# Decoder trunk on one core: the MoE blocks' gather and combine take fp32 operands whole, in place of two float32r pieces, and the table of extra passes is written early from ACT's queue

## What is computed

```python
scores = jax.nn.sigmoid((x @ router_w).astype(jnp.float32))
...
_, idx = lax.top_k(masked, TOP_K)
gate = jnp.take_along_axis(scores, idx, -1)
gate = gate / jnp.sum(gate, -1, keepdims=True) * ROUTED_SCALE
```

## Time and profile before

| | |
|---|---|
| median of 3 runs | 1443.56 us (1441.83 to 1446.32) |
| profiled execution, its own time | 1440.45 us |
| span of its trace | 1438.7 us |
| mean granted TensorE clock | 0.968 |
| PE busy | 1345.1 us, 93% of the span |
| DVE, ACT busy | 424.6 us, 317.4 us |
| DMA over the span | 310 GB/s, 446 MB |

### The profile page before, as it was taken

How to read it: one execution, slowest core, us unless ns; L and a number is a source line. 1 busy time by engine, 2 the same in 40 slices (tenths; PEclk the granted TensorE clock), 3 DMA queues, 4 the chain that set the end, 5 groups by cost and what they waited for, 6 DMA issues and landing times. The chain is left out here.

```text
span 1438.7 us, 16559 instructions
## 1 busy us (share of the span) xinstructions
PE 1345.1 (93%) x6265; PEld 672.7 (47%) x6265; DVE 424.6 (30%) x897; ACT 317.4 (22%) x670; POOL 18.2 (1%) x92
## 2 busy tenths in 40 slices
PE   7897889999999999999959879999999999999985
PEld 5665855343444434444325545544344343443432
DVE  2465527222221222212134234712212122121213
ACT  2354223111111111111112231311112111121111
POOL 1001000000000000000000000000000000000000
PEclk9998999999999999999989999999999999999997
DMA  9215025799999999999944522488999999999990
GB/s 348 91 36 206 1 77 215 283 376 397 418 417 417 419 416 419 417 418 418 415 169 154 191 109 97 195 337 364 408 417 418 418 417 419 418 417 419 416 383 32
DMA packets 93651, 446.24 MB, mean 310 GB/s; under 512 B 9972, under 2 KB 12455, under 8 KB 60327
## 3 DMA queue, kind: packets, MB, share of 16 engines
q1 hardware_dynamic: 93606, 445.64, 76.9%
HBM read 444.57 MB, written 1.05 MB: 310 GB/s over the span
## 5 line engine op out<-in xcount | busy, mean ns | idle before, releaser
L363 PE MATMUL psum<-w_up_ring,moe_x_selected 128*64 128x512 f32 x2048 | 455.0, 597 | 16.4 <-issue 16.4
L363 PEld LDWEIGHTS psum<-w_up_ring,moe_x_selected 128*64 128x64 f32 x2048 | 148.5, 138 | 311.0 <-issue 311.0
L426 PE MATMUL psum<-w_down_ring,moe_hT 128*64 128x512 f32 x1024 | 233.9, 598 | 0.9 <-ACT moe_hT L705 0.9
L887 DVE SCALAR_TENSOR_TENSOR moe_h<-moe_silu,moe_slot_gate,psum 128x256 f32<-128x256 f32 x64 | 30.7, 480 | 398.6 <-ACT moe_silu L698 398.6
L426 PEld LDWEIGHTS psum<-w_down_ring,moe_hT 128*64 128x64 f32 x1024 | 67.9, 136 | 134.4 <-issue 133.0
L698 ACT ACTIVATE moe_silu<-psum 128x256 f32<-128x256 f32 x64 | 24.6, 384 | 426.4 <-PE psum L363 426.4
L418 PE MATMUL psum<-moe_out_high,moe_matchT 128*128 128x512 f32 x256 | 113.9, 445 | 0.0
L905 DVE TENSOR_TENSOR moe_out_low<-psum,moe_out_high 128x512 fp32r<-128x512 f32 x64 | 44.3, 692 | 232.7 <-ACT moe_out_high L710 232.7
L376 PE MATMUL psum<-moe_match,moe_x_high 128*128 128x512 f32 x256 | 108.6, 424 | 0.0
L418 PE MATMUL psum<-moe_out_low,moe_matchT 128*128 128x512 f32 x256 | 101.3, 396 | 0.0
L376 PE MATMUL psum<-moe_match,moe_x_low 128*128 128x512 f32 x256 | 101.0, 395 | 0.0
(11 more groups left out here) (490 smaller groups left out, 1115.7 us busy)
## 6 DMA issues: line engine op xcount, KB each, us to landing
w_up_ring<-in_moe_w_gate SPq DMA_DIRECT2D x128, 1024.0 KB, 11.2
w_up_ring<-in_moe_w_up SPq DMA_DIRECT2D x128, 1024.0 KB, 13.3
w_down_ring<-in_moe_w_down SPq DMA_DIRECT2D x128, 1024.0 KB, 12.6
w_up_ring<-in_ev_w_in SPq DMA_DIRECT2D x4, 2048.0 KB, 12.2
w_up_ring<-in_od_w_in SPq DMA_DIRECT2D x4, 2048.0 KB, 10.4
w_up_ring<-in_ev_w_out SPq DMA_DIRECT2D x2, 2048.0 KB, 9.6
w_up_ring<-in_od_w_out SPq DMA_DIRECT2D x2, 2048.0 KB, 7.6
ln_gain_bias<-in_ln_g SPq DMA_DIRECT2D x4, 512.0 KB, 9.0
```

What stands on the lines that cost most here:

```text
L363: last = nc.tensor.matmul(k.psum[e * SLOTS:(e + 1) * SLOTS, 6, :], xsel[:, kk, own:own + SLOTS], up_view(slots[e], kk), start=kk == 0, sto ...
L426: last = nc.tensor.matmul(k.psum[e * SLOTS:(e + 1) * SLOTS, bank, :], hT[:, j * P + e * SLOTS:j * P + (e + 1) * SLOTS], k.w_down[slots[e]] ...
```

## The change

The pieces go. Gather reads `k.x` itself, every eighth column of a row of 1024 as the operand of 128 columns, and `match` becomes fp32. Combine reads one fp32 tile `y`, whose first half ACT copies out of bank 4 and whose second half DVE copies out of bank 7, each as soon as its own half of `pe_down` is done. `matchT` becomes fp32. `high_part` and `low_part` are dropped. The table is written to DRAM from ACT's DMA queue after the first pair, and read back from the same queue after the second; SP only waits for it where it did before. The loops for extra passes change in the same way and are left out here.

```diff
@@ pe_gather
-                for part in (x_high, x_low):
-                    last = nc.tensor.matmul(k.psum[:, 4 + kk % 2, :], part[:, t, kk, :],
-                                            match[:, t, :, :].rearrange("p e s -> p (e s)"),
-                                            start=t == 0 and part is x_high, stop=t == NT - 1 and part is x_low)
+                last = nc.tensor.matmul(k.psum[:, 4 + kk % 2, :], k.x[:, t, kk:D:KD],
+                                        match[:, t, :, :].rearrange("p e s -> p (e s)"), start=t == 0, stop=t == NT - 1)
@@ pe_combine
-            for o in (high, low):
-                last = nc.tensor.matmul(k.psum[:, 2 * t + half, :], matchT[:, i, t * P:(t + 1) * P],
-                                        o[:, half * BANK:(half + 1) * BANK], start=begin and o is high, stop=True,
-                                        skip_group_check=True)
+            last = nc.tensor.matmul(k.psum[:, 2 * t + half, :], matchT[:, i, t * P:(t + 1) * P],
+                                    y[:, half * BANK:(half + 1) * BANK], start=begin, stop=True, skip_group_check=True)
@@ sync
-            sp.wait_ge(s.table_sb, 1)
-            sp.dma_start(k.over_dram, table_i[:]).then_inc(s.table_dram, 16)
-            sp.wait_ge(s.table_dram, 16)
-            sp.dma_start(back_i[:].rearrange("p b c -> p (b c)"),
-                         k.over_dram.rearrange("b c -> (b c)").unsqueeze(0).to_broadcast([P, MAX_OVER * 4])
-                         ).then_inc(s.table_back, 16)
             sp.wait_ge(s.table_back, 16)
@@ tensor
-            pe.wait_ge(s.parts, NT)
             pe.wait_ge(s.match, 1)
             pe_gather(0, NT)
@@ tensor, pair
-                    pe.wait_ge(s.low_a, p)
-                    pe.wait_ge(s.low_b, p)
+                    pe.wait_ge(s.out_a, p)
+                    pe.wait_ge(s.out_b, p)
@@ scalar
-            high_part(0)
             take_xT(1)
             scores(0)
-            high_part(1)
             scores(1)
@@ scalar, pair
-                nc.scalar.copy(high[:, 0:BANK], k.psum[:, 4, :]).then_inc(s.high_a, 1)
-                act.wait_ge(s.down_b, p + 1)
-                nc.scalar.copy(high[:, BANK:], turn_ps).then_inc(s.high_b, 1)
+                nc.scalar.copy(y[:, 0:BANK], k.psum[:, 4, :]).then_inc(s.out_a, 1)
 
-            for i in range(4):
+            pair(0, 0, first=True)
+            act.wait_ge(s.table_sb, 1)
+            act.dma_start(k.over_dram, table_i[:]).then_inc(s.table_dram, 16)
+            pair(0, 1, first=True)
+            act.wait_ge(s.table_dram, 16)
+            act.dma_start(back_i[:].rearrange("p b c -> p (b c)"),
+                          k.over_dram.rearrange("b c -> (b c)").unsqueeze(0).to_broadcast([P, MAX_OVER * 4])
+                          ).then_inc(s.table_back, 16)
+            for i in (2, 3):
                 pair(0, i, first=True)
@@ vector
-            low_part(0)
             group_heads(0)
-            low_part(1)
             group_heads(1)
@@ vector, pair
-                dve.wait_ge(s.high_a, p + 1)
-                nc.vector.tensor_tensor(low[:, 0:BANK], k.psum[:, 4, :], high[:, 0:BANK], ALU.subtract).then_inc(s.low_a, 1)
-                dve.wait_ge(s.high_b, p + 1)
-                nc.vector.tensor_tensor(low[:, BANK:], turn_ps, high[:, BANK:], ALU.subtract).then_inc(s.low_b, 1)
+                dve.wait_ge(s.down_b, p + 1)
+                nc.vector.tensor_copy(y[:, BANK:], turn_ps).then_inc(s.out_b, 1)
```

More of the change, by code:

```diff
@@ L309, in output_and_experts @@
     shared_w = at("shared_weights", [P, 2, KD, FE], F32, SHARED_OFFSET)
[L310 to L313, removed]
+    y = at("out", [P, D], F32, SHARED_OFFSET)
+    matchT = at("matchT", [P, 4, S], F32, SHARED_OFFSET + 4 * D)
+    hT = at("hT", [P, KF * P], F32, SHARED_OFFSET + 8 * D)
     shared_wd = k.mixT[:].rearrange("p (j c) t -> p j (c t)", j=KF)
@@ L344, in output_and_experts @@
     back_i = sb("back_i", [P, MAX_OVER, 4], I32)
-    back = at("back", [P, MAX_OVER, 4], F32, SHARED_OFFSET + 13 * D)
-    shifted = at("shifted", [P, NT, 2], F32, SHARED_OFFSET + 14 * D)
+    back = at("back", [P, MAX_OVER, 4], F32, SHARED_OFFSET + 9 * D)
+    shifted = at("shifted", [P, NT, 2], F32, SHARED_OFFSET + 10 * D)
     up_ps, turn_ps = k.psum[:, 6, :], k.psum[:, 7, :]
@@ L384, in pe_gather_two @@
             for t in range(NT):
[L385 to L388, removed]
+                last = nc.tensor.matmul(k.psum[:, bank, c * P:(c + 1) * P], k.x[:, t, 4 * (bank - 4) + c:D:KD],
+                                        match[:, t, 0:2, :].rearrange("p e s -> p (e s)"), start=t == 0, stop=t == NT - 1)
         return last
@@ L614, in _ @@
             shared_down(1, 0)
-            pe.wait_ge(s.low_a, PAIRS)
-            pe.wait_ge(s.low_b, PAIRS)
+            pe.wait_ge(s.out_a, PAIRS)
+            pe.wait_ge(s.out_b, PAIRS)
             with pe.If(n_over < 1):
@@ L643, in _ @@
                     pe_down((2, 3), 1, 7).then_inc(s.v_down, 1)
-                    pe.wait_ge(s.v_low, 2 * i + 2)
+                    pe.wait_ge(s.v_out_a, i + 1)
+                    pe.wait_ge(s.v_out_b, i + 1)
                     pe_combine(0, 0)
@@ L663, in take_xT @@
                                    k.psum[:, 4 + b, :].rearrange("p (c n) -> p c n", c=4)).then_inc(s.xT, 1)
-            def high_part(t):
-                act.wait_ge(s.normed1, t + 1)
-                nc.scalar.copy(x_high[:, t], k.x[:, t, :].rearrange("p (c k) -> p k c", k=KD)).then_inc(s.x_high, 1)
             def scores(t):
@@ L733, in _ @@
                     act.wait_ge(s.v_down, i + 1)
-                    nc.scalar.copy(high[:, 0:BANK], k.psum[:, 4, :]).then_inc(s.v_high, 1)
-                    nc.scalar.copy(high[:, BANK:], turn_ps).then_inc(s.v_high, 1)
+                    nc.scalar.copy(y[:, 0:BANK], k.psum[:, 4, :]).then_inc(s.v_out_a, 1)
             nc.scalar.activation(w.early[:], w.ln_eps[:], ACT.Sqrt)
@@ L778, in _ @@
                 scale_shifted(nc, k, w1, t).then_inc(s.normed1, 1)
-            def low_part(t):
-                dve.wait_ge(s.x_high, t + 1)
-                dve.wait_ge(s.normed1, t + 1)
-                nc.vector.tensor_tensor(x_low[:, t], k.x[:, t, :].rearrange("p (c k) -> p k c", k=KD), x_high[:, t],
-                                        ALU.subtract).then_inc(s.parts, 1)
             def group_heads(t):
@@ L946, in _ @@
                                                    ALU.mult).then_inc(s.v_h, 1)
-                    dve.wait_ge(s.v_high, 2 * i + 2)
-                    nc.vector.tensor_tensor(low[:, 0:BANK], k.psum[:, 4, :], high[:, 0:BANK], ALU.subtract).then_inc(s.v_low, 1)
-                    nc.vector.tensor_tensor(low[:, BANK:], turn_ps, high[:, BANK:], ALU.subtract).then_inc(s.v_low, 1)
+                    dve.wait_ge(s.v_down, i + 1)
+                    nc.vector.tensor_copy(y[:, BANK:], turn_ps).then_inc(s.v_out_b, 1)
             dve.wait_ge(s.tables, 32)
```

10 lines of the change are left out of this document (4 added, 6 removed).

## The result

The changed kernel takes **1612.09 us**, the median of 4 runs (1611.05 to 1613.57). The kernel before took 1442.69 beside it (4 runs, 1440.41 to 1446.32). The ratio is **1.1172**, 95% interval 1.1146 to 1.1198: slower by 11.7%. The forecast of 1606 was 6 us low, and the range of 1592 to 1630 holds the time.

What follows compares the result with a forecast made beforehand. PE was taken to bound the kernel, with the DMA only just following. Gather +93.3, combine +92.8, router -0.4 and block ends -16.4 and -4.6 sum to +164.7 on a 1438.7 us span; forecast 1606 us, range 1592 to 1630.

Steps and rivals of the forecast that it cites:

- PE sets the pace: Steady MoE loop: PE, full through a 59.87 us cycle, is the bound; the DMA at 420 GB/s only just follows.
- Rival 4: MoE loop: the DMA sets the pace, so added PE work partly vanishes in hidden waits; 1590 us with a tenth gone; chance 0.05.
- Gather, +93.3: Gather: 16 fp32 matmuls of 0.859 us plus 0.1 fill, 13.84 against 8.01 us; 16 gathers add 93.3 us.
- Combine, +92.8: Combine: two fp32 halves take 3.60 us a pair against 2.15; over 64 pairs this adds 92.8 us.
- The router's choice, -0.4: Ahead of the router's choice: dropping high_part and low_part saves 0.2 us a layer, 0.4 in all.
- The ends of the blocks, -16.4 and -4.6: Last pair's pe_up in each block: the early table removes 16.4 us of idle time and 4.6 us of slow clock.
- The doubt that the last weights would be late: Block ends: weights still coming until about 1400 might be late next; the whole gain was taken, other bound 12 us.
- rival 3: Block ends: the gain stays out because PE waits for last weights or ACT's queue; about 1626 us; chance 0.06.
- ACT, 0: ACT's queue in the first quad: the table's write lands before the silu of pair 2, so the move costs 0.
- Rival 1: Gather and combine: fp32 records run at the pieces' pace, 0.25 us, giving about 1419 us; chance 0.02.
- Rival 2: Gather: strided weight loads of 32-byte step take up to 748 ns, adding 163 us, about 1769 us; chance 0.04.
- The sum: Whole kernel: 93.3 + 92.8 - 0.4 - 16.4 - 4.6 = +164.7 us of span.

Runs made afterwards that it cites:

- whole_packed: Changed kernel, but gather reads x from a packed fp32 copy made on ACT, so weight loads are contiguous: 1612.38 us.
- pieces_early_table: Kernel before with only the table moved, written and read back early on ACT's queue; gather and combine keep float32r pieces: 1419.50 us, ratio 0.9831.
- pieces_strided: Kernel before with x's two float32r pieces in x's own order, so gather loads every eighth column: 1450.83 us, ratio 1.0057.

## Why the prediction was right, step by step

**PE sets the pace.** Right. After the change PE is busy for all 72.08 us of a cycle and the DMA at 0.87. Rival 4 fell: no part of the added work went into hidden waits, since the halves' 6.04 and 6.16 add up to the cycle's 12.21.

**Gather, +93.3.** The mechanism was right, two records of 0.43 us for each fp32 product; the size was slightly off. A gather takes 14.06 us and not 13.84, so 14 of them cost 6.05 more each. The first of each block costs 5.39 more (242.41 to 250.84 before, 242.44 to 256.26 now). Together 95.5, and the kernel with gather's edit alone has 95.4. The 0.22 that was missed lies at a gather's start. The first gather of a block, whose first load begins 0.43 us ahead of its first record (242.01 and 242.44), takes 13.82 us, 0.08 over 32 records. The others start behind `pe_up` with load and record together and take 0.24 more, or 0.11 more where the loads are packed (whole_packed, 13.93). So the strided load accounts for 0.13 of it; the forecast's 0.1 for filling the array stood for all the rest, which is 0.19.

**Combine, +92.8.** This was the term that missed most. The halves came as forecast (1.82 and 1.81, so 3.63 against a forecast 3.60), but the price of a pair was worked out from 2.15, the halves alone. From the start of combine to `pe_down` a pair took 1068.50 - 1065.98 = 2.52 and takes 1184.19 - 1180.11 = 4.08: +1.56, of which 1.48 in the halves and 0.08 in the transposes between them, which now take 0.45 instead of 0.37. Over a quad the mean is 6.16 / 4 = 1.54, and 64 pairs make 98.6, where the experiment has 99.2. I had let the work between the halves out of the sum because its instructions didn't change; its length did.

**The router's choice, -0.4.** The gain came, though the first gather starts at 242.44 us and started at 242.41 before. PE's timeline before, in the first block:

```profile
239.78 0.23 PE L528 MATMUL psum<-moe_sel_bf,before_bf 128*128 128x64 bf16 x2 [0.23 <-DVE moe_sel_bf L816]
...
242.41 0.80 PE L376 MATMUL psum<-moe_match,moe_x_high 128*128 128x512 f32 x1
243.05 0.40 PE L376 MATMUL psum<-moe_match,moe_x_low 128*128 128x512 f32 x1
```

and in the changed kernel:

```profile
239.41 0.22 PE L513 MATMUL psum<-moe_sel_bf,before_bf 128*128 128x64 bf16 x2
```

From the start of the shared expert's ten records to the choice PE took 5.96 us and takes 5.61; in the second block 5.73 and 5.57. Together that is 0.5 for the forecast 0.4. The cover was not whole: in the first block PE idled 0.23 us for DVE, which is gone. The first record of the old gather stands 0.64 us ahead of the second, where records come every 0.23, so its recorded start is some 0.4 early. That is why the gain doesn't show there, and why the first gathers seem to cost 5.39 and not 5.8: the gain is inside the 95.5.

**The ends of the blocks, -16.4 and -4.6.** Right: 21.0 forecast, and pieces_early_table has 21.5 by the span (23 to 26 by the medians, since the profiled execution of the kernel before is one of its fastest). Both `pe_up` are back at 7.04 us. The doubt that the last weights would be late was unfounded, even at the DMA's full pace. That the gain stays out (rival 3) fell. But the gain belongs to the kernel before: with combine whole, a late table costs 4 to 5 us only. Had I priced the change's two parts in the other order, products first, the table would have been worth 5 and the products would have cost 17 less (1614.2 - 1438.7 = 175.5 by the spans, not 192.8); the sum is the same, the story of what the table brings is not.

**ACT, 0.** Right. The silu waits for PE alone. The forecast allowed 15.8 us for the write, the time with 6 MB ahead of it in the queue; it took 3.9.

**Rival 1** (fp32 at the pieces' pace) fell with 0.43 us for a record. The rate that the Trainium skill's Perfetto Trace Analysis, section Engine Utilization, halves for one fp32 form is not that of a whole fp32 product here, which takes two such records. By the Trainium skill's FP8 and Floating Point Precision, section TensorE Precision Notes, true fp32 is four passes, and the trace agrees within 8%: 0.859 us over 4 is 0.215 for 512 columns, and a float32r record of the same shape comes every 0.23. **Rival 2** (the strided operand) fell as a mechanism with a price: the load is longer, 314 against 190 ns, but by the 0.13 of whole_packed only some 2 of the 171 us are its own. The penalty that the Trainium skill's SBUF — State Buffer, section Door 1: The DMA port swizzle, states for leaving a 16-byte line agrees with the load's length and hardly shows in the time.

**The sum**: 95.5 + 98.6 - 21.5 = +172.6, and the spans differ by 171.3. The sum charges 1.54 for the combine of each block's last pair too, but from the start of that pair's `pe_down` to the end of the block only 0.82 and 0.83 were added (738.51 to 756.34 and 1417.26 to the end before, 823.10 to 841.75 and 1587.73 to the end now). That is 1.4 less, as much as the 1.3 that the sum has too much. In the prediction, +164.7 was 6.6 us too little: 2.2 in gather and 5.8 in combine were missing and the 0.4 for the router is counted in gather's 95.5, less 0.5 at the ends and that 1.3.

The version to keep is neither kernel: pieces as before with the table sent early, 1419 us on either queue, 1.7% below the kernel before and 12% below the changed one.

## What to carry to other kernels

Price a slower operation from the start of the group to the start of the next unchanged one, not from the changed instructions alone: what stands between them is stretched too. A change of several parts should be run part by part, since one part (here a small DMA moved early, worth 21 us by itself) can hide behind another, and its worth depends on how far the queue behind it is in arrears. Where two resources are both full, shortening the work of one brings little until the other's is shortened too: here 71 us less of PE busy time brought 12.

## What the runs showed of the hardware

- An fp32 matmul of 128 x 512 shows as two records of 0.429 us from start to start, 0.859 together; a float32r one comes every 0.23. So fp32 costs 3.7 float32r matmuls, and 1.8 times a product in two float32r pieces (away from the changes of bank).
- A weight load of 128 fp32 elements at a step of 32 bytes is recorded with 314 to 334 ns, and with 190 packed. float32r records still come every 0.25 us under such loads (pieces_strided), against 0.23 with packed ones; so longer loads seem to overlap. Which part of a load does so, the trace doesn't say.
- A write of 0.5 KB landed 15.8 us after its issue behind the weights in SP's queue, 14.0, 11.1 and 10.8 where the backlog was smaller, 3.1 to 3.9 (medians of the two layers) on ACT's queue, with weights coming beside it for part of that time, and 1.3 on SP's queue with the DMA idle. The read-back of 64 KB took 2.8 us behind the last weights in SP's queue and 7.9 to 8.2 on ACT's queue beside weights (pieces_early_table and the changed kernel).
- The weights come at 417 to 421 GB/s on one core in the stretches where they are always asked for, at a share of 1.01 to 1.03.
